# Rotary turns of the attention's queries and keys on VectorE instead of TensorE

## The reference

```python
def _apply_rope(x, cos, sin):
    half = x.shape[-1] // 2
    xf = x.astype(jnp.float32)
    x1, x2 = xf[..., :half], xf[..., half:]
    c = cos[None, :, None, :]
    s = sin[None, :, None, :]
    return jnp.concatenate([x1 * c - x2 * s, x2 * c + x1 * s], axis=-1).astype(x.dtype)
...
    q = _apply_rope(q.reshape(B_, T_, ATT_HEADS, ATT_HD), cos_a, sin_a)      # 8 heads of 128
    k = _apply_rope(k.reshape(B_, T_, ATT_KV_HEADS, ATT_HD), cos_a, sin_a)   # 2 heads of 128
    qi = _apply_rope(qi.reshape(B_, T_, IDX_HEADS, IDX_HD), cos_i, sin_i)    # 8 heads of 64
    ki = _apply_rope(ki.reshape(B_, T_, 1, IDX_HD), cos_i, sin_i)[:, :, 0]   # 1 head of 64
```

## Time and profile before

| | |
|---|---|
| time, median of 3 executions | 1268.21 us (1267.95 to 1268.28) |
| span of the profiled execution | 1268.2 us |
| TensorE busy | 1254.3 us (99%), 9041 matmuls |
| VectorE busy | 919.6 us (73%) |
| ScalarE busy | 699.2 us (55%) |
| GpSimd busy | 154.3 us (12%) |
| mean granted clock of TensorE over the span | 0.998 |
| stretch from 129 to 170 us, with the rotations 3 to 8: TensorE, VectorE, ScalarE, GpSimd busy | 40.64, 32.69, 16.81, 9.77 us |

### The profile page before, as it was taken

The page is one execution under the profiler, slowest core; times in us unless marked ns, Lnnn a source line. Parts: engine busy times, 40 slices in busy tenths (PEclk is TensorE's granted clock), DMA queues, the critical chain, the costliest instruction groups (busy, mean ns, idle before and its releaser), DMA issues.

```text
span 1268.2 us, 23324 instructions
## 1 busy us (share of the span) xinstructions
PE 1254.3 (99%) x9041; PEld 1169.6 (92%) x9041; DVE 919.6 (73%) x1290; ACT 699.2 (55%) x1082; POOL 154.3 (12%) x113
## 2 busy tenths in 40 slices
PE   9999999999999999999999999999999999999998
PEld 8997999999989998889998989999889998999986
DVE  6886874878778774447734547999758777999954
ACT  5556465654456343345354546666547567766642
POOL 0000142000000000000000001642200000464310
PEclk9999999999999999999999999999999999999999
DMA  7552332322355555555553444555564444454562
GB/s 300 189 173 101 133 134 101 133 68 68 152 197 188 195 179 185 198 170 182 183 209 109 156 173 167 198 169 195 194 221 171 162 154 163 167 188 175 197 224 93
DMA packets 30315, 212.83 MB, mean 168 GB/s; under 512 B 3488, under 2 KB 3616, under 8 KB 5152
## 3 DMA queue, kind: packets, MB, share of 16 engines
q1 hardware_dynamic: 29088, 206.53, 46.9%
q0 software_dynamic: 1152, 5.24, 1.1%
HBM read 210.71 MB, written 1.05 MB: 167 GB/s over the span
## 4 chain that ended last, share of the span: by engine, by line
PE 86%; DVE 8%; ACT 4%; DMA 1%; issue 1%; SPq 0%; DVEq 0%; ACTq 0%
PE lin L540 50%; PE lin L702 21%; DVE wlo L513 3%; PE lin L2883 2%; PE lin L567 2%; ACT whi L506 2%; PE lin L569 1%; DMA raw<-in_stream 1%; PE aux L2627 1%; PE aux L2599 1%; PE aux L2485 1%; ACT lm L1377 1%; PE aux L725 1%; PE aux L2745 1%; PE aux L2555 1%
## 5 line engine op out<-in xcount | busy, mean ns | idle before, releaser
L513 DVE TENSOR_TENSOR wlo<-raw,whi 128x2048 fp32r<-128x2048 f32 x183 | 427.4, 2338 | 170.8 <-ACT whi L506 170.1
L506 ACT CAST whi<-raw 128x2048 fp32r<-128x2048 f32 x192 | 365.3, 1906 | 179.5 <-DMA raw<-in_stream 147.0
L540 PE MATMUL lin<-xhi,whi 128*128 128x256 f32 (+2 forms) x1616 | 461.5, 286 | 1.0 <-DVE wlo L513 1.0
L540 PE MATMUL lin<-xlo,whi 128*128 128x256 f32 (+2 forms) x1616 | 457.0, 283 | 0.0
L540 PE MATMUL lin<-xhi,wlo 128*128 128x256 f32 (+2 forms) x1616 | 454.7, 281 | 0.0
L540 PEld LDWEIGHTS lin<-xhi,whi 128*128 128x128 f32 x1616 | 304.1, 188 | 3.0 <-DVE wlo L513 1.2
L540 PEld LDWEIGHTS lin<-xhi,wlo 128*128 128x128 f32 x1616 | 306.1, 189 | 0.0
L540 PEld LDWEIGHTS lin<-xlo,whi 128*128 128x128 f32 x1616 | 304.6, 189 | 0.4
L865 POOL TENSOR_TENSOR fu<-fs,ft 128x256 f32<-128x256 f32 x44 | 86.2, 1958 | 259.4 <-ACT fs L1479 259.4
L2292 DVE SCALAR_TENSOR_TENSOR ft<-fy,par,ft 128x254 f32<-128x254 f32 (+1 forms) x176 | 109.5, 661 | 5.9 <-DVE ft L2292 0.2
L540 PE MATMUL lin<-whi,xhi 128*128 128x256 f32 x256 | 74.2, 290 | 0.0
(11 more groups left out here) (454 smaller groups left out, 2123.2 us busy)
## 6 DMA issues: line engine op xcount, KB each, us to landing
raw<-in_stream SPq DMA_DIRECT2D x193, 1024.0 KB, 4.9
gp<-in_gains POOLq DMA_DIRECT2D x6, 512.0 KB, 3.9
c<-in_const SPq DMA_DIRECT2D x1, 1460.0 KB, 16.0
h<-in_x SPq DMA_DIRECT2D x2, 544.0 KB, 4.4
c<-in_const POOLq DMA_DIRECT2D x1, 1024.0 KB, 6.5
ht<-in_xtok POOLq DMA_DIRECT2D x1, 1024.0 KB, 9.6
out<-ht SPq DMA_DIRECT2D x1, 512.0 KB, 2.6
out<-ht SPq DMA_DIRECT2D x2, 256.0 KB, 2.0
```

The source lines that it names most:

```text
L506: nc.scalar.copy(whi[:, s0 % 4], raw[:, s0 % 4]).then_inc(hi_ready, 1)
L513: nc.vector.tensor_tensor(wlo[:, s0 % 4], raw[:, s0 % 4], whi[:, s0 % 4].bitcast(F32), ALU.subtract).then_inc(lo_ready, 1)
L540: ins = nc.tensor.matmul(out, a, b, start=start and n == 0, stop=stop and n == 2)
```

## The change

The rotations 3 to 8 (two key heads, four pairs of query heads) lose TensorE's product. VectorE multiplies partitions 0 to 63 of x by the sine table and writes to partitions 64 to 127 of `ctmp`, then partitions 64 to 127 of x to partitions 0 to 63; the sine table `sina` has its upper half negated, so that the sign is right. The cosine product and the sum stay as they are. VectorE waits for ScalarE's copy of the projection where it waited for TensorE's product. The matrix `turna` leaves the constants (128 columns of float32, 64 KB), so that the buffers behind them lie 512 bytes lower, and the rotations 3 to 8 take no bank of `aux`, so that those behind them are dealt other banks. The rotations 0 to 2 of the index heads, whose halves are 32 features, stay on TensorE.

```diff
         for step in PROJECT:
             if step[0] == "rot":
-                use_next(ROT[step[1]])
+                if step[1] < 3:
+                    use_next(ROT[step[1]])
...
-        use_next(ROT[8])
...
+            def rotate_halves(step):
+
+                name, x, W, c, sn, t0 = todo[step]
+                n = x.shape[1]
+                pair_done(dve, pair_first["ak"] if step < 5 else pair_first["aq"] + step - 5)
+                for lo, hi in ((0, 64), (64, 0)):
+                    ins = nc.vector.tensor_tensor(ctmp[hi:hi + 64, 0, 0:n, 0:W], x[lo:lo + 64],
+                                                  bc(cst(sn, lo=t0, n=W)[lo:lo + 64], n), ALU.mult)
+                own.link(ins)
+                own.link(nc.vector.tensor_tensor(x, x, bc(cst(c, lo=t0, n=W), n), ALU.mult))
+                nc.vector.tensor_tensor(x, x, ctmp[:, 0, 0:n, 0:W], ALU.add).then_inc(S("rope"), 1)
+                dve.wait_ge(S("rope"), step + 1)
+
             def rotate(step):
+                if step > 2:
+                    rotate_halves(step)
+                    return
...
             for step in PROJECT:
                 if step[0] == "rot":
-                    rotation(step[1])
+                    if step[1] < 3:
+                        rotation(step[1])
...
-            gate_part(0, 0, 2)
-            rotation(8)
-            gate_part(0, 2, 5)
+            gate_part(0, 0, 5)
             pe.wait_ge(S("rope"), 9)
...
+        if tag == "a":
+            c["sina"][P // 2:] *= -1.0
+            continue
```

More of the change, by code:

```diff
@@ L71 @@
 CONST1 = [("ident", 128), ("window", 32), ("upper", 128), ("upper16", 128), ("ones16", 128), ("spread", 128), ("head", 8),
-          ("levels", 4 * 128), ("cosa", T1), ("sina", T1), ("cosi", T1), ("sini", T1), ("turna", 128),
+          ("levels", 4 * 128), ("cosa", T1), ("sina", T1), ("cosi", T1), ("sini", T1),
           ("turni", 128), ("past", 2 * T1)]
@@ L393, in use_next @@
                 turn_at[0] += 1
-        ROT = ["rot_ik", "rot_iq0", "rot_iq1", "rot_ak0", "rot_ak1"] + [f"rot_aq{n}" for n in range(4)]
+        ROT = ["rot_ik", "rot_iq0", "rot_iq1"]
         for step in PROJECT:
             if step[0] == "rot":
-                use_next(ROT[step[1]])
+                if step[1] < 3:
+                    use_next(ROT[step[1]])
             elif step[0] == "idx":
@@ L2379, in rotation @@
                 name, x, W, c, sn, t0 = todo[step]
-                turn = cst("turni" if c == "cosi" else "turna")
+                turn = cst("turni")
                 if name == "rot_ik":
                     pair_done(pe, 0)
-                elif name[:6] == "rot_iq":
+                else:
                     pair_done(pe, pair_first["iq"] + int(name[6:]))
[L2385 to L2388, removed]
                 b = fill(name)
```

## The result

The changed kernel takes 1271.55 us (median of 6 executions, 1271.32 to 1273.24), the kernel before 1268.08 us beside it (1267.46 to 1268.30). The ratio is 1.0031, with a 95% interval of 1.0021 to 1.0042: 3.5 us slower.

The account below looks back on a forecast made before the run. TensorE is busy 99% of the span, but before the logits it waits for VectorE's last rotation. 1268.2 plus 1.4 us of VectorE lateness plus 1.7 us of lower TensorE clock gave 1271.3 us, range 1268.7 to 1272.9.

Parts of the forecast that it names:

- What is late: Before the attention's logits, VectorE's last rotation is late; TensorE's saved 4.36 us turn idle, its wait growing to 6.15 us.
- The first term, +1.43 us: Logits start 1.43 us later, as VectorE's four query rotations take 2.90 us each instead of 2.18.
- the walk: VectorE followed from 137.24 through key rotations, weighted sums, rotation 5, rounds and last three rotations, ending at 166.15.
- lower walk: The same path of VectorE with half products at 0.61 and 0.35 us, ending at 165.60: +0.86 us.
- The key rotations at nothing: The two key rotations' extra half products fit VectorE's 1.75 us of idle time before the index scores' weighted sums.
- The price from both sides: A VectorE half product costs 0.61 to 0.72 us for a query, 0.35 to 0.47 for a key; upper ends taken.
- the rival in which a half product costs half: VectorE's half products cost 0.36 us, logits start at 163.2, total 1266.6 to 1268.2 us; chance 0.05.
- The clock, +1.7 us: TensorE's clock falls in the long wait before the logits, costing 1.7 us behind it, bounds 0 and 2.8.
- What is late next: nothing: Behind the logits' start, gate slots, exponentials and loads move along; nothing there takes the delay back.
- The sum: Whole kernel: 1268.2 + 1.4 + 1.7 = 1271.3 us, 0.25% slower.
- That the clock holds: TensorE's clock before the logits doesn't fall or costs under 1.1 us, total 1269.1 to 1270.7 us; chance 0.34.
- That TensorE's time counts after all: The logits aren't held by the ninth rotation, so TensorE's 4.36 us come out: 1263.9 us; chance 0.03.

Follow-up runs that it names:

- experiment 3: The changed kernel with both half products of a rotation reading and writing partitions 0 to 63, so the rotation isn't computed: 1271.25 us, ratio 1.0024.
- Experiment 1: The changed kernel with 24 small products, result unused, on TensorE ahead of its wait for the ninth rotation: 1269.59 us, ratio 1.0013.
- experiment 2: The kernel before with only the two key rotations (3 and 4) by half products on VectorE: 1267.46 us, ratio 0.9998.
- experiment 5: The changed kernel with 7 gate pieces ahead of TensorE's wait, half of slot 1's low part made early and slot 3's low part on GpSimd: 1265.34 us, ratio 0.9981.
- experiment 7: The changed kernel with 12 small products, result unused, on TensorE ahead of its wait for the ninth rotation: 1271.57 us, ratio 1.0025.
- experiment 4: The changed kernel with 9 more gate pieces ahead of TensorE's wait, slot 1's whole low part made early and ScalarE's gate copies before its exponentials: 1267.08 us, ratio 0.9995.
- experiment 6: The kernel before, all rotations on TensorE, with gate pieces, low parts and copies reordered to put gate work ahead of the ninth rotation's wait: 1269.17 us, ratio 1.0010.

## Why the prediction was right, step by step

**What is late.** Right. TensorE's wait for the last rotation was to be 6.15 us and is 6.31. TensorE's last matmul ahead of it ends 30.74 us behind the transposes (157.87 + 0.28 - 127.41); I had 160.02 - 129.21 = 30.81. So the 4.36 us were well priced, and all of them turned into idle time (6.31 - 0.36 = 5.95, of which 4.43 were taken from TensorE by these rows and 1.52 are lateness).

**The first term, +1.43 us.** It measures +1.52. I took the upper end for a half product, 0.72 and 0.47 us, and it is 0.70 and 0.45 (1.39 / 2 and 0.89 / 2 in the rows, with 0.03 behind each pair). Shifted to this execution, 1.80 us earlier by the transposes, the walk forecast the weighted sums at 139.2, the low part at 141.44, rotation 5 at 143.64, the first round at 146.54 and the last three rotations at 155.65. They stand at 139.29, 141.53, 143.85, 146.72 and 155.82. The largest slip is a step of 0.12 us: from the start of the low part to rotation 5 it is 2.32 us (141.53 to 143.85) and not 2.20, since a half product that writes to other partitions doesn't overlap the low part either. In experiment 3, where it writes to the same ones, these are 2.20 us. The prediction priced the change of partitions between the two halves and not the one in front of the first. It also mixed two starting points: its lower walk gives 165.60 - 164.74 = 0.86, its upper one by the same count 166.15 - 164.74 = 1.41 and not 1.43. Experiment 1, in which only this term is left, lies 1.6 us above the kernel before.

**The key rotations at nothing.** Right: the weighted sums start without idle time in the changed kernel and in experiment 2.

**The price from both sides.** The lower end was wrong, and experiment 3 shows why: two half products overlap only on the same partitions. Even there the two take 1.28 us and not half of it, so the rival in which a half product costs half is out.

**The clock, +1.7 us.** It measures 2.0 us in the medians (1271.55 against 1269.59 with the filler) and 2.31 in the profile (8.83 against 6.52). The mechanism was right and the size a little short. That it came so near is in part luck: 1.7 was a choice within bounds of 0 and 2.8 us, not worked out. I had taken the stretch of 3.42 us seen elsewhere and rounded it up; here 4.88 us of work ran at half speed, and 21 matmuls started in them where 37 did in the 4.86 us behind the same start before, which gives 4.88 x (1 - 21/37) = 2.1 us.

**What is late next: nothing.** Right, with 951.7 us behind the last products with `tu` and `al` for 951.9. In the changed kernel TensorE waits for nothing else up to 185 us, and GpSimd's low parts follow the ninth rotation as before.

**The sum.** 1271.3 forecast, 1271.55 measured. The differences add up to 1.52 + 2.31 = 3.8 in the profiles, 3.5 in the medians. The two terms, 3.1 us, were 0.4 short of the medians, and 0.1 us came back because the kernel before was 1268.08 us this time. One thing under the sum was weaker than I knew: that the span of the profiled execution equals the median time was a coincidence. In every run in which both are known the time lies 1.7 to 2.1 us above the span (after: 1271.65 and 1269.9; experiment 5: 1266.01 and 1264.2), and the 54 executions of the kernel before that were timed beside the experiments have spans of 1265.6 to 1267.3 us, against the 1268.2 that I read. So the execution whose profile I read was longer than most. The fall of the clock at 122.48, 1.4 us, fits that: the changed kernel's profile and those of experiments 1 to 6 haven't got it at that place (only that of experiment 7 has). The changed kernel's row there:

```profile
120.68:124.10 3.42, 3.42 (x30) 3.27 (x31) 2.90 (x13) 2.34 (x6) 0.00 (x0) 1.00 0.00 0
```

The forecast added differences to 1268.2 as a time, and as a time it is the median. The difference of the two profiled spans, 1269.9 - 1268.2 = 1.7 us, would have shown only half of the loss.

**The rivals.** That the clock holds: against it the stretches above, and experiment 1, which is what this rival looks like when it is made true: 1269.59, within its 1269.1 to 1270.7. That TensorE's time counts after all: not in this order of work. Experiments 5 and 6 show what it needs, 2.8 us of real work moved from behind the wait to before it.

## What to carry to other kernels

An engine that is busy 99% of the time isn't thereby the one that sets the end at each place: where its one wait is for the engine that is to take over the work, moving the work makes the busy engine idle and the kernel slower by what the other one gets, here 1.5 us for 4.4 us saved. An idle stretch on TensorE has a second price behind it, in the matmuls that then run at half speed (2.0 us here), and filler that covers most of the wait or, better, real work from behind it takes it away. So judge such a move together with a new order of the work: alone it lost 3.5 us, with gate pieces moved in front of the wait it gained 2.8.

## What the runs showed of the hardware that I had not expected

- A VectorE instruction with two inputs in SBUF didn't finish beside a GpSimd subtraction until that had ended: 1.60 us for 0.44 in experiment 4 and 0.58 for 0.44 in experiment 6, ending 0.30 and 0.31 us behind GpSimd. The maxima, which read one tensor, and the replacements, whose eight values an instruction of their own loads (MATCH_VALUE_LOAD in the trace), ran beside it at their usual 0.45 and 0.43 us. So engines don't meet only at semaphores. That the second input decides was not tested by itself. The Trainium skill (SBUF — State Buffer, section SBUF: two separate sides) has it that the two engines share a pair of ports that one instruction holds as a whole, also against a VectorE instruction with two inputs in SBUF. These runs agree.
- In the traces the clock fell after 3.6 us of idle time as well as in one of 6.3, and in experiment 7 it fell 0.6 us after TensorE had begun to work again. So half the filler saved 0.7 us of the 2.3 in the trace (8.14, 8.83 and 6.52 us from the logits to the same gate matmul), and nothing in the medians (1271.57 us against 1271.55).
